# Two chained transformer blocks: the first tile's copies put ahead of the second tile's squares, a bias split put behind the last weight split, four bias matmuls put between transposes, and weight slots freed earlier

## The reference

```python
for i in range(2):
    h = rms_norm(x, g[0])
    m = parallel_conv_mla(h, ...) if i == 0 else conformer_conv(h, ...)
    x = x + rms_norm(m, g[1])
    h = rms_norm(x, g[2])
    x = x + rms_norm(squared_relu_mlp(h, mlp_w1[i], mlp_w2[i]), g[3])
```

## Time and profile before

| | us |
|---|---|
| median of 3 runs | 923.44 (922.0 to 924.53) |
| the profiled execution | 923.78 |
| its span, first to last instruction | 922.0 |
| PE busy in the span | 901.8 |
| DVE busy | 689.9 |
| ACT busy | 268.9 |
| POOL busy | 284.0 |

### The profile page before, as it was taken

How to read it: one execution, slowest core, us unless ns; L and a number is a source line. 1 busy time by engine, 2 the same in 40 slices (tenths; PEclk the granted TensorE clock), 3 DMA queues, 4 the chain that set the end, 5 groups by cost and what they waited for, 6 DMA issues and landing times.

```text
span 922.0 us, 13057 instructions
## 1 busy us (share of the span) xinstructions
PE 901.8 (98%) x4934; PEld 756.7 (82%) x4934; DVE 689.9 (75%) x725; ACT 268.9 (29%) x550; POOL 284.0 (31%) x182
## 2 busy tenths in 40 slices
PE   8999999999999999999999999999999999999997
PEld 6987788888887787688888888888867888888886
DVE  5779879777777775769877777669787687676774
ACT  3537441111112511342111111455586411111112
POOL 5100055444442332136444443200000243333331
PEclk9999999999999999999999999999999999999999
DMA  8851625655558265216655555366502356556641
GB/s 290 283 204 79 219 85 200 226 182 182 182 195 276 99 208 183 92 46 228 201 200 198 200 200 178 107 226 215 219 1 81 104 196 216 190 179 211 192 137 46
DMA packets 82376, 160.29 MB, mean 174 GB/s; under 512 B 5065, under 2 KB 40667, under 8 KB 82337
## 3 DMA queue, kind: packets, MB, share of 16 engines
q1 hardware_dynamic: 82176, 159.68, 50.5%
q10 hardware_dynamic: 160, 0.07, 0.0%
HBM read 158.68 MB, written 1.05 MB: 173 GB/s over the span
## 4 chain that ended last, share of the span: by engine, by line
PE 85%; DVE 8%; ACT 3%; issue 2%; POOL 1%; DMA 1%; DVEq 0%; SPq 0%; POOLq 0%; ACTq 0%
PE ps L1930 82%; PE ps L1934 3%; DVE w_lo L750 2%; ACT arena L1480 1%; DMA x_res<-in_x 1%; ACT w_hi L1476 1%; POOL st L638 0%; ACT arena L1831 0%; DVE nrm L839 0%; DVE st L1292 0%; DVE act_hl L1101 0%; DVE x_res L836 0%; ACT arena L1627 0%; POOL st L637 0%; DVE arena L1416 0%
## 5 line engine op out<-in xcount | busy, mean ns | idle before, releaser
L750 DVE TENSOR_TENSOR w_lo<-raw,w_hi 128x2048 fp32r<-128x2048 f32 (+3 forms) x140 | 325.9, 2354 | 40.0 <-POOL w_hi L731 21.7
L1930 PE MATMUL ps<-act_hl,w_hi 128*128 128x512 f32 (+1 forms) x1088 | 242.0, 369 | 3.6 <-DVE act_hl L909 2.6
L1930 PEld LDWEIGHTS ps<-act_hl,w_hi 128*128 128x128 f32 x1088 | 183.7, 191 | 33.8 <-issue 3.6
L1930 PE MATMUL ps<-w_hi,hl 128*128 128x512 f32 (+2 forms) x680 | 186.7, 384 | 0.6 <-DVE w_lo L750 0.6
L617 POOL TENSOR_SCALAR w_hi<-raw 128x2048 fp32r<-128x2048 f32 x56 | 137.3, 2452 | 157.3 <-PE ps L1930 148.5
L1930 PE MATMUL ps<-w_hi,act_hl 128*128 128x512 f32 (+3 forms) x656 | 181.1, 381 | 2.4 <-DVE w_lo L750 2.4
L1930 PEld LDWEIGHTS ps<-w_hi,hl 128*128 128x128 f32 (+1 forms) x680 | 125.7, 189 | 24.0 <-issue 0.8
L1930 PEld LDWEIGHTS ps<-act_hl,w_lo 128*128 128x128 f32 x1024 | 135.9, 190 | 8.4 <-DVE w_lo L750 0.3
L1930 PEld LDWEIGHTS ps<-w_hi,act_hl 128*128 128x128 f32 x656 | 118.6, 188 | 27.0 <-issue 4.1
L1930 PE MATMUL ps<-act_hl,w_lo 128*128 128x256 f32 (+1 forms) x1024 | 139.4, 281 | 0.0
L1930 PE MATMUL ps<-w_lo,hl 128*128 128x512 f32 (+1 forms) x356 | 108.4, 378 | 0.0
(11 more groups left out here) (212 smaller groups left out, 741.0 us busy)
## 6 DMA issues: line engine op xcount, KB each, us to landing
raw<-in_mlp_w SPq DMA_DIRECT2D x64, 1024.0 KB, 5.2
raw<-in_w_gate SPq DMA_DIRECT2D x22, 512.0 KB, 3.9
raw<-in_w_up SPq DMA_DIRECT2D x22, 512.0 KB, 4.9
raw<-in_w_down SPq DMA_DIRECT2D x11, 1024.0 KB, 5.0
raw<-in_odd_w_pw SPq DMA_DIRECT2D x16, 512.0 KB, 5.4
raw<-in_w_in SPq DMA_DIRECT2D x8, 1024.0 KB, 6.1
raw<-in_even_w_in SPq DMA_DIRECT2D x6, 1024.0 KB, 5.6
raw<-in_even_w_out SPq DMA_DIRECT2D x4, 1024.0 KB, 6.8
```

Of the source, the lines that this page charges most:

```text
L750: tt(w_lo[slot_of(n)][:, 0:w], raw[slot_of(n)][:, 0:w], w_hi[slot_of(n)][:, 0:w].bitcast(F32), ALU.subtract).then_inc(S("w_split"), 1)
L1930: return pe.matmul(o, l, r, start=start, stop=stop, skip_group_check=True)
```

## The change

It does the following, from top to bottom:
- POOL: the root of tile 1 waits for two more of ACT's squares and for one of DVE's only, and comes after `hi(1)` instead of before it.
- DVE: the square of tile 1 is gone from the opening.
- DVE: `bias_low(0)` comes after the low part of the last piece.
- ACT: tile 0's copies come before tile 1's squares; both halves of tile 1's squares are on ACT.
- PE: the four `bias_pw2` matmuls come between the two transposes of k = 4.
- PE: `narrow(0, 1, True)` and `narrow(1, 1, True)` come directly behind `narrow(0, 1, False)` and `narrow(1, 1, False)`, each with its count on `pe_piece`; `tall` on piece n+4 starts with the high weights and waits for the low ones in its second part.

```diff
@@ POOL @@
-                    gp.wait_ge(S("first_sq"), m + 1)
-                    gp.wait_ge(S("second_sq"), m + 1)
+                    gp.wait_ge(S("first_sq"), 2 * m + 1)
+                    gp.wait_ge(S("second_sq"), 1)
...
                 first_rsqrt(0)
-                hi_until(0)
+                hi_until(1)
                 first_rsqrt(1)
@@ DVE @@
                 first_norm(0)
-                first_square(1)
                 first_low(0)
                 first_norm(1)
                 lo_until(0)
...
                     hidden_lo(MLP_BLOCKS - 1, act_hl)
+                    lo_until(n0 + 4 * MLP_BLOCKS - 1)
                     if s == 0:
-                        lo_until(n0 + 4 * MLP_BLOCKS - 2)
                         bias_low(0, bias_pw1)
-                    lo_until(n0 + 4 * MLP_BLOCKS - 1)
@@ ACT @@
-                for m in range(M):
-                    act.wait_ge(S(f"x_in{m}"), 16)
-                    f(junk[:, m, 0:512], x[:, m, 0:512], ACT.Square, ...)
-                act.wait_ge(S("gain_col"), 1)
-                for m in range(M):
+                def first_square(m, h):
+                    f(junk[:, m, 512 * h:512 * h + 512], x[:, m, 512 * h:512 * h + 512], ACT.Square, ...)
+                def first_high(m):
                     for k0 in range(0, KD, TILE_STEP[m]):
...
+                act.wait_ge(S("x_in0"), 16)
+                first_square(0, 0)
+                act.wait_ge(S("gain_col"), 1)
+                first_high(0)
+                act.wait_ge(S("x_in1"), 16)
+                first_square(1, 0)
+                first_square(1, 1)
+                first_high(1)
@@ PE @@
                                 pe.wait_ge(S("normed_1"), k // 4 + 1)
+                            if m == 1 and k == 4:
+                                for b in range(4):
+                                    mm(ps[:, ACC + b, :], sel[:, b % 2, :], bias_pw2, True, False)
...
-                for m in range(M):
-                    for h in range(2):
-                        mm(ps[:, ACC + 2 * m + h, :], sel[:, h, :], bias_pw2, True, False)
...
                         narrow(j, m, False)
+                        if m == 1 and j < 2:
+                            narrow(j, 1, True).then_inc(S("pe_piece"), 1)
                 lows[0] += TILE_LOWS
-                for j in range(4):
-                    if j >= 2:
-                        arrived(n + j)
-                        narrow(j, 0, True)
+                for j in range(2, 4):
+                    arrived(n + j)
+                    narrow(j, 0, True)
                     narrow(j, 1, True).then_inc(S("pe_piece"), 1)
...
-                    tall(n + 4 + q, UP, act_hl, 2 * q, q == 0, q == 3, 2, 1024)
+                    tall(n + 4 + q, UP, act_hl, 2 * q, q == 0, q == 3, 2, 1024, low_last=q == 0)
```

More of the change, by code:

```diff
@@ L1536, in high_of_turned @@
                         act_high(turned(bank, 2 * j, 2), 2 * j, 2)
-                for m in range(M):
-                    act.wait_ge(S(f"x_in{m}"), 16)
-                    f(junk[:, m, 0:512], x[:, m, 0:512], ACT.Square, scale=1.0 / D ** 0.5, accum_out=ssx[:, 2 * m:2 * m + 1])\
-                        .then_inc(S("first_sq"), 1)
-                act.wait_ge(S("gain_col"), 1)
-                for m in range(M):
+                def first_square(m, h):
+                    f(junk[:, m, 512 * h:512 * h + 512], x[:, m, 512 * h:512 * h + 512], ACT.Square, scale=1.0 / D ** 0.5,
+                      accum_out=ssx[:, 2 * m + h:2 * m + h + 1]).then_inc(S("first_sq"), 1)
+                def first_high(m):
                     for k0 in range(0, KD, TILE_STEP[m]):
```

## The result

Five executions of the changed kernel took 926.79 to 927.91 us, median 927.55; the median before is 923.44. The ratio is 1.0047, its 95% interval 1.0036 to 1.0059: the change costs about 4.1 us, 0.4%. The forecast was 925.4, with a range of 920.8 to 927.3: the result lies 2.15 above it and 0.25 above the range. The profiled execution took 927.91, 4.13 more than the one of before, and its span 926.1, 4.1 more. The table takes both profiles apart, from the start of one group of PE's transposes to that of another (us).

What follows compares the result with a forecast made beforehand. PE, busy for 98% of the span, was taken as the bound. Opening +4.3, end of first MLP -1.2, bias matmuls -0.3 and slots -0.8 sum to +2.0 us: median 923.44 becomes 925.4, range 920.8 to 927.3.

Steps and rivals of the forecast that it cites:

- the term for the clock: Opening, tile 1: after PE's 3.4 us idle, 32 matmuls run at the low clock; +1.5 us, bounds 0 and 3.0.
- Rival 3: Opening: blocks as forecast, clock low for all of tile 1's work; 3.0 instead of 1.5, 926.9 us; chance 0.17.
- the block: Opening: POOL's copies hold up DVE's scaling and `lo(0)` at shared SBUF ports; tile 1's matmuls start 2.8 us later.
- the three later places: End of first MLP, layer norm's transposes and `w_in_2`: PE's stalls shrink or go; -1.2, -0.3 and -0.8 us.
- Rival 1: Opening: `hi(3)` comes too late to get in, `lo(0)` ends at 19.4; 923.0 us; chance 0.22.
- Rival 2: Opening: no block at all, PE starts on tile 1 at 20.0, -0.5 us; total 920.6; chance 0.13.
- The start of PE's work: Opening, tile 0: PE's first matmul at 10.88 instead of 12.03, 1.15 us earlier.
- The bias split: End of first MLP: low part comes before the bias split, shortening PE's 1.63 us wait; -1.2, bounds -1.63 and -0.6.
- The turned bias matmuls: Layer norm: bias matmuls between transposes let `tall` start at 381.25 instead of 381.55; -0.3 us, bounds -0.5 and +0.2.
- `w_in_2`: Slots freed sooner let ACT copy piece n+4 earlier, so PE's 0.78 us stall goes; -0.8, bounds -0.8 and -0.3.
- The lock: Opening: the skill's exclusive-port rule would end the scaling's first half at 16.48 + 0.44, 0.15 us later than the row.

Runs made afterwards that it cites:

- POOL waiting: Changed kernel with one wait more: POOL copies piece 2 only when DVE has scaled tile 1; 922.25 us, ratio 0.9987.
- root first: Changed kernel with POOL's old order in the opening, the root of tile 1 ahead of the copy of piece 1; 927.01 us, ratio 1.0046.
- bias later: Changed kernel with the old opening and the bias split moved into the boundary, behind the first two gains; 921.99 us, ratio 0.9986.
- best: Changed kernel with the old opening, 13 blank matmuls instead of 4 there, and the bias split behind `post_gain(0)`; 922.1 us, ratio 0.9988.
- the opening alone: Kernel before with only the opening's edits on POOL, DVE and ACT; 929.47 us, ratio 1.0066.
- the two on `w_in_2`: Kernel before with one edit each: early low matmuls alone, or high weights first in `tall` alone; the stage took 75.48 and 75.49 us.
- The two experiments with a wait: Changed kernel with POOL waiting for DVE's scaling of tile 1 before copying piece 2, or before piece 3 only; 922.25 and 925.18 us.

## Why the prediction was wrong

**The step that failed is the term for the clock.** The forecast took 1.5 for one low stretch behind PE's idle time, the price of the one in before, and nothing for the clock anywhere else. In the profile the low clock cost 2.74 in the opening and 1.61 in the attention. The 2.74 are two terms: the 16 low matmuls took 3.67 - 1.98 = 1.69 more, and tile 1's 32 matmuls 5.12 - 4.07 = 1.05 more. In before the stretch was 3.4 us long, here 6.8. That the clock would fall, and where, was right; that one more idle stretch costs what the last one did was not worked out from anything, though the bounds went to 3.0. Rival 3, with 3.0 for this term, sat nearest: 2.74 is beyond the 2.3 from which it was to decide.

**The attention was not in the sum, and it is the larger share.** The miss of the profile, 4.16 against 2.0, is 1.24 for the clock in the opening, 1.61 for the attention, 0.61 less for the block (4.93 - 2.74 leaves 2.19 of the 2.8), and 0.08 less for the three later places together. With the opening's errors alone the median would have been forecast at about 926.0, inside the range; the stretch in the attention carries it beyond. The forecast gave no reason for putting it at nothing.

Its cause stays open. No instruction moved there, and the opening does not decide it: profiles of variants have the low stretch there in four cases (POOL waiting, root first, bias later, best) and not in the other six, with the new and with the old opening alike. But these four and after all have the three later edits together. Of the eight profiles with all of them five have the stretch, and of the four without (before, the opening alone, the two on `w_in_2`) none. The executions lean the same way: 9 of the 33 of the three kernels with the old opening and all later edits have a mean clock of 0.996 or less, against 3 of 55 of before. So it can be a cost of the later edits rather than chance, and no experiment separates the two. The result does not hang on it alone: three of after's five executions are at 0.993 to 0.994 and took 927.55 to 927.91, the two at 0.995 took 926.79 and 926.86, which is inside the forecast's range and still 3.4 above the median before.

**The block was right in mechanism, and 0.6 too large in size.** `lo(0)` ended at 20.86 (forecast 21.2), PE stood at the low matmuls until 20.92 (21.3). Only the order was another: `hi(3)` asked at 16.5, not 16.85, early enough to get in between the two halves of the scaling (4.12 for both) rather than ahead of `lo(0)`, which took 2.27 and not 4. Rival 1 wanted it too late, and it came too early. The two experiments with a wait make 1.6 to 1.7 for each copy, where the forecast had 2.28 of DVE's time as the whole of what POOL's `hi(2)` lost in before; the rows say 4.02 - 1.90 = 2.12.

**Rival 2's gain was the clock's.** Without a block tile 1's matmuls start at 19.47, where it said 20.0 and the profile of before has 20.51. But 1.49 of that is the low clock in before, with which the rival compared a start at full clock; with the clock up in both, the new opening is 0.62 behind the old one. The start of PE's work was forecast at 10.88 and came at 11.33, and at 10.99 to 11.61 in the variants with this opening: the distance from the first transpose, 3.15 here, is nearly the 3.09 worked out, but the ten blank matmuls ahead of the transposes took 2.63, so these started later than 7.79.

**The later places.** The bias split gave -1.10 (-1.2), and here the size is partly luck. The forecast left 0.4 of the old wait, since POOL's copy was to block the split; two splits took 4.48, unblocked, and no wait is left. It had DVE late by 0.15 at the boundary, and 0.78 of wait appeared at the transposes. The two errors nearly cancel. The turned bias matmuls gave -0.21 (-0.3). `w_in_2` gave -1.07 (-0.8), the stall being worth more than its idle time. That either of its two edits does it alone was said, and holds.

**The lock.** The first half of the scaling ended 0.28 behind POOL's end where only `hi(2)` was in its way (14.57 + 2.49 - 0.39 = 16.67, against 14.51 + 1.88 = 16.39), as in before. The Trainium skill (SBUF — State Buffer, Who interferes with whom) calls it an exclusive lock in which the other blocks fully. The trace agrees that the later one is done only behind the other's end, and puts the time after the release at 0.28 and not the 0.44 of a whole instruction. It would change this sum by 0.15.

## What to carry to other kernels

Before an edit makes one engine start early, find which chain sets the next start and work out the gain at equal clocks (here it lost 0.6 even without the block). Don't let a release that POOL gives to DVE be followed at once by a long POOL instruction on SBUF; one wait there was worth 5.3 us of median, the clock's part included. Where one profile is compared with another, read the granted clock of every stage first. When a forecast prices the low clock, it needs a term for every stage in which the clock may fall and not only for the one that is changed; here the stage left out cost 1.61 of the 2.16 missed.

## What the runs showed of the hardware

- DVE and POOL take turns. With three copies in a row on POOL and three instructions in a row on DVE, each of DVE's took place behind one of POOL's (4.14 for two that take 0.88, 3.94 for one that takes 2.28). Where DVE had the access first, POOL's two copies took 5.70 instead of 3.8; `lo(0)` lost nothing then (2.29), and the next split took 3.75 instead of 2.28.
- A small instruction is held up as a large one is: POOL's part of a root on 128 x 1 values took 1.39 instead of 0.36 beside DVE's bias split of 1.22.
- A few hundredths of a us in the start go with the order. POOL had it where its copy started 0.04 to 0.06 ahead (14.00 and 14.04, 14.49 and 14.54, 14.51 and 14.57). DVE had it at a distance of 0.03 or less, whichever of the two started first (14.20 and 14.20, 14.15 and 14.16, 14.30 and 14.27; POOL's start is named first in each pair).
- The stretches at 1.2 GHz lasted 3.4, 6.8 and 10.2 us in the openings seen, and root first had two of 3.4 apart from each other. The same opening with nearly the same idle time ahead (2.33 to 2.38) had one in two profiles and none in the third. A stretch of 3.4 us cost 1.5 in the opening and 1.6 in the attention.
- A stall of 0.78 in brackets cost 1.07 to 1.10.
